# Four 512-token norms worked in two token halves of 256, with the matmuls on either side of them

## The chip, the cores and the metric

The kernel runs on one core of one Trainium2 chip. Inside the core several engines work side by side, each through its own queue of instructions: PE (TensorE: matmuls, with its weight loads shown apart as PEld), DVE (VectorE), ACT (ScalarE), POOL (GpSimd) and SP (SyncE, which issues transfers). They hold each other up only through semaphores. The metric is the time of one execution on the device in microseconds (us); lower is better. The time before is the median of three executions. The profile is of one further execution and has its own, slightly different time.

## The reference

Two blocks run one after the other. The change lies in the second, a trunk of two layers over 256 latent tokens and 256 context tokens, 512 columns in all:

```python
def half_ffn(x, m, name):
    sh, sc, g = m
    h = modulate(rms_norm_2(x, prm[name + "_norm"]), sh, sc)     # h * (1 + sc) + sh
    return x + 0.5 * g * swiglu(h, prm[name + "_w_in"], prm[name + "_w_out"])

def trunk_layer(xl, xc, ...):
    xl = half_ffn(xl, mod_l[0:3], "ffn1");  xc = half_ffn(xc, mod_c[0:3], "ffn1")
    hl = modulate(rms_norm_2(xl, prm["mix_norm"]), mod_l[3], mod_l[4])     # hc the same way
    ol, oc = mixer(hl, hc, ...)                                  # projections, attention, w_out
    xl = xl + mod_l[5] * ol
    xl = half_ffn(xl, mod_l[6:9], "ffn2")                        # xc the same way in layer 0
```

A norm needs the sum of squares of a token's 1024 features before any feature of that token can be scaled. Shift and scale differ between the latent and the context tokens.

## The kernel before

Activations are kept as eight tiles of 128 features by 512 tokens, `x[:, k, :]`. A product is made in three passes over rounded operands: high by high, low by high, high by low. So each weight piece of 128 by 128 costs three matmuls for each of its contraction steps, and both a weight piece and an input tile have to be split first: ACT rounds (`w_hi`, `h_hi`), then DVE takes the difference (`w_lo`, `h_lo`). Weights pass through a ring of four pieces; a piece may be rounded when the piece four places earlier has been multiplied. Accumulators are eight PSUM banks, used in turn.

An FFN works in two halves of its hidden width. Each half first multiplies 22 input pieces (8 contraction steps each) and then 8 output tiles o0 to o7 (11 steps each, three matmuls of 512 columns per step: L1233 to L1235). DVE adds each finished output tile to x (L2368), in two operations of 256 columns. After the last output tile comes the next stage, through a norm:

- ACT squares each x tile (L1581, the last tile in two halves at L1576). PE adds the squares up over features with a column of ones, in small matmuls (`norm_sums`, L991): tiles 0 to 2 after o5, tiles 3 and 4 after o6, the rest after o7. The two accumulators of these sums lie in the banks of o0 and o1.
- For each token half, ACT takes the root (L1589), DVE the reciprocal (L2049), and PE spreads the result over the 128 partitions (`spread_half`, L809, from `rs`).
- DVE multiplies x by it (L2125, halves apart). ACT writes the rounded modulated tile (`h_hi`, L1670) and the unrounded one (L1676), two operations of 256 columns each and one wait for both. DVE subtracts (`h_lo`, L2149).
- PE multiplies the first four weight pieces of the next stage tile by tile as these arrive, 8 steps, three matmuls of 512 columns each, 96 in all: `first_pieces` (L1260, L1261, L1265) where an FFN follows, `first_features` (L875, L876, L878) where a mixer's projections follow. Tiles 0 and 1 come first for all pieces; at the end each piece takes its last steps alone, so piece 0 closes 18 matmuls before the end.
- The weights of pieces 2 and 3 are rounded by ACT in the middle of the modulation (`ahead(2)`, `ahead(3)`; L1742, in the mixers L1648) and split by DVE (L2341, L2183). Piece 4 takes piece 0's place in the ring. In an FFN, ACT's queue has ahead of it a load of an activation table and the SiLU of piece 0's result (L1754); in a mixer, two copies out of PSUM (L1896) and two squares.

Four norms of 512 tokens stand between tiles in this way, in this order of time: "b2.0.nm" (FFN 1 of layer 0, then the mixer), "b2.0.n2" (the mixer's output projection, with 8 steps per tile, then FFN 2), "b2.1.n1" (FFN 2 of layer 0, then FFN 1 of layer 1) and "b2.1.nm" (FFN 1 of layer 1, then its mixer). They are called norms 1 to 4 here. All queues are written out by hand; no scheduler orders them.

Of the kernel before, what the change touches and what calls it, by code (L numbers as in the profile page):

```python
# [196 lines left out]
def columns(items):  # L197
# [26 lines left out]
    "attended", "combined", "copied", "exponentiated", "piece_multiplied", "gated",  # L224
# [91 lines left out]
def program(nc, book, weights, d_const, d_late, d_param, d_cond, d_x, d_ctx, d_bias, d_out):  # L316
# [13 lines left out]
    with ExitStack() as ctx:  # L330
# [33 lines left out]
        mscale = sb("mscale", [P, KD, 2])  # L364
        warm = sb("warm", [P, 1])
# [3 lines left out]
        (attended, combined, copied, exponentiated, piece_multiplied, gated,  # L369
# [217 lines left out]
        NORM_N = {nm: SEQ if nm in ("b1.0", "b1.1", "b2.1.n2") else TOK for nm in BEFORE}  # L587

# [193 lines left out]
        def _(pe):  # L782
# [70 lines left out]

            def first_features(names, rhs, N):
# [183 lines left out]
            def norm(nm, summed_before=0):  # L1038
# [6 lines left out]
                for h in range(halves):  # L1045
                    if E.new(f"{nm}.root.{h}"):
                        pe.wait_ge(*E.at(f"{nm}.root.{h}"))
                    spread_half(f"{nm}.rs.{h}", banks[h], rs, h, SEQ // GROUPS * h)

# [169 lines left out]
            def ffn(nm, nn, N, then=None):  # L1219
# [48 lines left out]

                x_hi, x_lo = [h_hi[:, k, 0:N] for k in range(KD)], [h_lo[:, k, 0:N] for k in range(KD)]
                u_hi, u_lo = [hidden_hi[:, k, 0:N] for k in range(KH)], [hidden_lo[:, k, 0:N] for k in range(KH)]  # L1270
                for half in range(2):
                    tile = tile_number(nm, half)
                    if half == 0:
                        first_pieces()
# [15 lines left out]
                    for o in range(KD):  # L1290
# [6 lines left out]
                        ready = [3 * (tile + k + 1) for k in range(KH)] if o == 0 else None  # L1297
                        piece(half, 2 * KH + o, u_hi, u_lo, ready)
                        if half and then and o in (5, 6):
                            if o == 5:  # L1300
                                state["bank"] = piece_number(nm, 1, 2 * KH) % BANKS
                                for i in range(2):
                                    occupant[(state["bank"] + i) % BANKS] = f"{nm}_o1.{i}"
                            norm_sums(then, range(3) if o == 5 else range(3, 5))
                for o in range(2 * bool(then), KD):
                    q = piece_number(nm, 1, 2 * KH + o)
                    occupant[q % BANKS] = f"{nm}_o1.{o}"
# [125 lines left out]
            norm("b2.0.nm", 5)  # L1433
            rhs = normed("b2.0.nm", TOK)
            state["rotating"] = 7
            for j in range(7):
# [9 lines left out]
                if j == 0:  # L1446
                    first_features([f"b2.0.in.{i}" for i in range(4)], rhs, TOK)
# [44 lines left out]
            for j in range(4):  # L1492
# [3 lines left out]
                if j == 2:  # L1496
                    norm_sums("b2.0.n2", range(4))
            norm("b2.0.n2", 4)
            ffn("b2.0.ffn2", "b2.0.n2", TOK, "b2.1.n1")
            norm("b2.1.n1", 5)  # L1500
# [1372 lines left out]
```

## Time and profile before

| quantity | value |
| --- | --- |
| median of three executions | 2490.09 us (2485.32 to 2491.04) |
| profiled execution, its own time | 2493.8 us |
| span of the profiled execution, first to last instruction | 2492.0 us |
| PE busy | 2417.2 us, 97% of the span |
| DVE busy | 1668.9 us, 67% |
| ACT busy | 993.5 us, 40% |
| DMA | 358.71 MB, mean 144 GB/s |
| mean granted clock of TensorE | 0.979 of full speed |

The profiled execution is 3.7 us above the median, and 1.8 us of it lie outside the span. PE's busy time counts a matmul that runs at a lower granted clock, and one that is stretched by its neighbours, as busy; the share by itself doesn't tell how fast PE works.

### The profile page before, as it was taken

How to read it: one execution, taken by the hardware profiler on the slowest of the kernel's cores; microseconds unless marked ns; L12 is line 12 of the kernel's file. 1: busy time of each engine (PE TensorE's matmuls, PEld its weight loads, DVE VectorE, ACT ScalarE, POOL GpSimd, SP SyncE). 2: the span in 40 equal slices, each digit the busy share in tenths (PEclk: the TensorE clock that was granted, in tenths of full speed). 3: DMA queues.
4: the chain of work that ended last, by engine and by line, in shares of the span. 5: the costliest groups of instructions: out<-in, count | busy, mean ns of one | idle time of the engine just before them, and what ended most of it. 6: DMA issues, size and time to landing. Idle time of an engine off the chain costs nothing.

```text
span 2492.0 us, 38157 instructions
## 1 busy us (share of the span) xinstructions
PE 2417.2 (97%) x15684; PEld 2068.4 (83%) x15684; DVE 1668.9 (67%) x2598; ACT 993.5 (40%) x1493; POOL 50.6 (2%) x72
## 2 busy tenths in 40 slices
PE   8999999999999999999999999999999999998999
PEld 7989899998988888876457888887888887967999
DVE  5589875789868688644864866854856853465654
ACT  5347545366562222252464321225221224455432
POOL 0000000000000000000030000000000000020000
PEclk9999999999999999999989999999999999999999
DMA  7644345544435355413102434432434531502553
GB/s 262 206 168 138 122 148 193 195 173 139 156 109 209 122 201 193 153 68 108 68 1 102 172 135 176 186 126 102 186 131 181 191 115 63 165 18 102 178 188 109
DMA packets 66717, 358.71 MB, mean 144 GB/s; under 512 B 15472, under 2 KB 20720, under 8 KB 30192
## 3 DMA queue, kind: packets, MB, share of 16 engines
q1 hardware_dynamic: 66544, 356.27, 40.0%
q8 instruction: 124, 2.03, 0.3%
q14 instruction: 49, 0.40, 0.0%
HBM read 351.82 MB, written 1.05 MB: 142 GB/s over the span
## 4 chain that ended last, share of the span: by engine, by line
PE 89%; DVE 5%; ACT 3%; issue 1%; POOL 1%; SPq 0%; DMA 0%; DVEq 0%; ACTq 0%; POOLq 0%
PE psum L1233 16%; PE psum L1235 16%; PE psum L1234 16%; PE psum L809 7%; PE psum L846 7%; PE psum L848 7%; PE psum L847 6%; DVE slab L2331 2%; PE psum L924 1%; PE psum L930 1%; PE psum L925 1%; PE psum L1156 1%; PE psum L955 1%; PE psum L957 1%; PE psum L956 1%
## 5 line engine op out<-in xcount | busy, mean ns | idle before, releaser
L1742 ACT ACTIVATE w_hi<-wring 128x1024 fp32r<-128x1024 f32 (+1 forms) x240 | 273.4, 1144 | 531.1 <-PE psum L1235 423.0
L1233 PE MATMUL psum<-h_hi,w_hi 128*128 128x512 f32 (+1 forms) x1280 | 464.4, 363 | 0.7 <-DVE w_lo L2341 0.7
L1234 PE MATMUL psum<-h_lo,w_hi 128*128 128x512 f32 (+1 forms) x1280 | 464.0, 363 | 0.0
L1235 PE MATMUL psum<-h_hi,w_lo 128*128 128x512 f32 (+1 forms) x1280 | 464.0, 363 | 0.0
L2341 DVE TENSOR_TENSOR w_lo<-wring,w_hi 128x1024 fp32r<-128x1024 f32 (+1 forms) x240 | 318.4, 1329 | 151.3 <-ACT w_hi L1742 150.9
L2210 DVE CUSTOM_DVE_ANT_0 products<-wring,cond,prm 128x1024 bf16<-128x1024 f32 x288 | 369.5, 1283 | 7.8 <-DMA wring<-in_w_mod 0.6
L846 PE MATMUL psum<-h_hi,w_hi 128*128 128x256 f32 (+1 forms) x1176 | 355.1, 302 | 10.8 <-issue 8.7
L848 PE MATMUL psum<-h_hi,ring_lo 128*128 128x256 f32 (+1 forms) x1176 | 350.2, 298 | 0.0
L847 PE MATMUL psum<-h_lo,w_hi 128*128 128x256 f32 (+1 forms) x1176 | 349.5, 297 | 0.0
L2183 DVE TENSOR_TENSOR ring_lo<-wring,w_hi 128x1024 fp32r<-128x1024 f32 x208 | 247.2, 1223 | 138.7 <-ACT w_hi L1648 136.5
L1233 PEld LDWEIGHTS psum<-h_hi,w_hi 128*128 128x128 f32 x1280 | 241.6, 189 | 39.1 <-DVE w_lo L2341 1.9
L1234 PEld LDWEIGHTS psum<-h_lo,w_hi 128*128 128x128 f32 x1280 | 241.6, 189 | 37.4
L1235 PEld LDWEIGHTS psum<-h_hi,w_lo 128*128 128x128 f32 x1280 | 241.6, 189 | 37.4
L1233 PE MATMUL psum<-hidden_hi,w_hi 128*128 128x512 f32 (+1 forms) x704 | 255.9, 364 | 0.0
L1234 PE MATMUL psum<-hidden_lo,w_hi 128*128 128x512 f32 (+1 forms) x704 | 255.3, 363 | 0.0
L1235 PE MATMUL psum<-hidden_hi,w_lo 128*128 128x512 f32 (+1 forms) x704 | 255.2, 363 | 0.0
L1648 ACT ACTIVATE w_hi<-wring 128x1024 fp32r<-128x1024 f32 x208 | 211.1, 1053 | 108.7 <-PE psum L848 35.7
L846 PEld LDWEIGHTS psum<-h_hi,w_hi 128*128 128x128 f32 x1176 | 223.4, 190 | 30.1 <-issue 22.6
L847 PEld LDWEIGHTS psum<-h_lo,w_hi 128*128 128x128 f32 x1176 | 224.9, 191 | 6.2
L848 PEld LDWEIGHTS psum<-h_hi,ring_lo 128*128 128x128 f32 x1176 | 224.2, 191 | 6.8
L1754 ACT ACTIVATE squares<-psum 128x512 f32<-128x512 f32 (+1 forms) x88 | 47.9, 544 | 289.9 <-PE psum L1235 289.9
L1233 PEld LDWEIGHTS psum<-hidden_hi,w_hi 128*128 128x128 f32 x704 | 132.9, 189 | 21.0
(211 smaller groups left out, 3525.3 us busy)
## 6 DMA issues: line engine op xcount, KB each, us to landing
wring<-in_w_b_ffn_in SPq DMA_DIRECT2D x80, 1024.0 KB, 6.9
wring<-in_w_mod SPq DMA_DIRECT2D x72, 1024.0 KB, 4.9
wring<-in_w_b_ffn_out SPq DMA_DIRECT2D x64, 704.0 KB, 4.1
wring<-in_w_b_merge SPq DMA_DIRECT2D x24, 1024.0 KB, 4.8
wring<-in_w_b_out SPq DMA_DIRECT2D x16, 1024.0 KB, 4.8
wring<-in_w_b_in SPq DMA_DIRECT2D x16, 1024.0 KB, 5.2
wring<-in_w_b_q SPq DMA_DIRECT2D x12, 1024.0 KB, 6.3
wring<-in_w_b_k SPq DMA_DIRECT2D x12, 1024.0 KB, 5.0
```

The costliest lines, as they stand in the source:

```text
L809: return nc.tensor.matmul(out, lhsT, rhs, start=(k == 0), stop=(k == n - 1))
L846: nc.tensor.matmul(out, mixer_hi(q)[:, k, :], r_hi, start=(k == 0), stop=False)
L847: nc.tensor.matmul(out, mixer_hi(q)[:, k, :], r_lo, start=False, stop=False)
L848: mm = nc.tensor.matmul(out, lo[:, k, P * t:P * t + P], r_hi, start=False, stop=(k == len(rhs) - 1))
L1233: nc.tensor.matmul(acc, wh[:, k, :], rhs_hi[k], start=(k == 0), stop=False)
L1234: nc.tensor.matmul(acc, wh[:, k, :], rhs_lo[k], start=False, stop=False)
L1235: return nc.tensor.matmul(acc, wl[:, k, :], rhs_hi[k], start=False, stop=(k == n - 1))
L1648: A(mixer_hi(q), slot_of(c).rearrange("p (k n) -> p k n", n=256)[:, :, P * i:P * i + P], ACT.Copy).then_inc(weights_rounded, 1)
L1742: A(part_piece(w_hi, q, i), raw_piece(c, i), ACT.Copy).then_inc(weights_rounded, 1)
L2183: V.tensor_tensor(mixer_lo(c)[:, :, P * i:P * i + P], raw, mixer_hi(q).bitcast(F32), ALU.subtract).then_inc(weights_split, 1)
L2210: V.tensor_tensor_reduce(out=products[:, :], in0=slot_of(c)[:, D * t:D * t + D], in1=cond[:, g, :], scale=1.0, scalar=R(f"b2.{l}.mod_b", 2 ...
L2341: V.tensor_tensor(part_piece(w_lo, q, i), raw_piece(c, i), part_piece(w_hi, q, i).bitcast(F32), ALU.subtract).then_inc(weights_split, 1)
```

## The change

The last two output tiles ahead of each of the four norms, the norm, and the first four pieces behind it are worked in two halves of 256 tokens. For each of the norms:

- `last_halves` multiplies o6 and o7 for the first token half, then both for the second, with matmuls of 256 columns (L1130 to L1132). The accumulators hold a half of both tiles each, instead of one tile.
- The sums of squares of tiles 0 to 2 still follow o5, but their accumulators now take the banks of o4 and o5. Tiles 3 to 5 follow the first half of o6. `late_sums` (tiles 6 and 7 of one half) and `spread_root` for the first token half are put into the second half's matmuls, after 12 and 27 of them (24 in norm 2).
- `first_halves` multiplies the first four pieces for the first token half (L1164, L1165, L1167): pieces 0 to 2 step by step, then piece 3 alone. Into it go `late_sums` for the second half after step 2, and `spread_root` for it after step 4. Then follows the second token half in the old order of steps.
- ACT and DVE have `halved_norm` in place of `norm` and `modulate`, and `norm` and `scaled`. Each operation covers one half, with a wait of its own. ACT's squares and root of the second half stand among its operations of the first.
- A separate tile `mgate` keeps the gate factors, which shared `mscale` before.

PE has 630 matmuls more than before: 162 for each of norms 1, 3 and 4, 144 for norm 2.

```diff
+        def halved_base(nm):
+            if nm == "b2.0.n2":
+                return piece_number("b2.0.ffn2", 0) % BANKS
+            return piece_number(HALVED[nm], 1, 2 * KH) % BANKS
+        def halved_banks(nm):
+            free = [(halved_base(nm) + i) % BANKS for i in range(KD - 2)]
...
+            return free[0:PARTS], free[PARTS:]
...
+            def early_sums(nm, some):
+                if some[0] == 0:
+                    state["sum"] = [take(f"{nm}.sum.{h}", fixed=halved_banks(nm)[1][h]) for h in range(2)]
...
+            def last_halves(nm, pieces, accs):
+                for h in range(2):
+                    for p, (w_h, w_l, r_hi, r_lo, close) in enumerate(pieces):
+                        n = len(r_hi)
+                        out = accs[h][:, half_of(p)]
+                        for k in range(n):
+                            nc.tensor.matmul(out, w_h[k], r_hi[k][:, half_of(h)], start=(k == 0), stop=False)
+                            nc.tensor.matmul(out, w_h[k], r_lo[k][:, half_of(h)], start=False, stop=False)
+                            mm = nc.tensor.matmul(out, w_l[k], r_hi[k][:, half_of(h)], start=False, stop=(k == n - 1))
...
+                            if (h, p, k) == (0, 0, n - 1):
+                                early_sums(nm, range(3, KD - 2))
+                            if (h, p, k) == (1, 0, 3):
+                                late_sums(nm, 0)
+                            if (h, p, k) == (1, 0, min(8, n - 1)):
+                                spread_root(nm, 0)
+            def first_halves(nm, lands, weights_of, acc_of, close):
+                first = []
+                for k in range(KD + 1):
+                    first += [(k, i, 0) for i in range(PARTS - 1) if k < KD] + [(k - 1, i, 1) for i in range(PARTS - 1) if k]
+                first += [(k, PARTS - 1, part) for k in range(KD) for part in range(2)]
+                for h, order in enumerate((first, first_passes(TOK))):
...
+                        if (h, k, i, part) == (0, 2, PARTS - 2, 1):
+                            late_sums(nm, 1)
+                        if (h, k, i, part) == (0, 4, PARTS - 2, 1):
+                            spread_root(nm, 1)
...
-                        if half and then and o in (5, 6):
-                            if o == 5:
-                                state["bank"] = piece_number(nm, 1, 2 * KH) % BANKS
...
-                            norm_sums(then, range(3) if o == 5 else range(3, 5))
+                        if half and then and o == 5:
+                            early_sums(then, range(3))
...
+                    last_halves(then, last, [psum[:, piece_number(nm, 1, 2 * KH + o) % BANKS, :] for o in (KD - 2, KD - 1)])
...
+            def halved_norm(nm, l, which, ahead):
...
+                for k in range(KD):
+                    high_and_plain(k, 0)
+                    if k == 1:
+                        ahead(2)
+                    if k == 4:
+                        square(KD - 2, 1)
+                        square(KD - 1, 1)
+                        ahead(3)
+                    if k == 5:
+                        root_half(1)
+                for k in range(KD):
+                    high_and_plain(k, 1)
```

The first place at which rows are shown is PE's queue after output tile o5, ahead of norm 3; L991 and L1030 are the sums of squares, and a name in brackets is a semaphore that the row waits for. Before:

```order
L1235 MATMUL psum<-hidden_hi,w_lo 128x512
L991 MATMUL psum<-squares,cst 32x64 [waits rooted,ffn_added]
L991 MATMUL psum<-squares,cst 32x64 x7
L991 MATMUL psum<-squares,cst 32x64 [waits rooted]
L1233 MATMUL psum<-hidden_hi,w_hi 128x512 [waits weights_split,gated]
L1234 MATMUL psum<-hidden_lo,w_hi 128x512
```

After:

```order
L1360 MATMUL psum<-hidden_hi,w_lo 128x512
L1030 MATMUL psum<-squares,cst 32x64 [waits rooted,ffn_added]
L1030 MATMUL psum<-squares,cst 32x64 x7
L1030 MATMUL psum<-squares,cst 32x64 [waits rooted]
L1130 MATMUL psum<-hidden_hi,w_hi 128x256 [waits hidden_written,weights_split,gated]
L1131 MATMUL psum<-hidden_lo,w_hi 128x256
```

The place of the sums is the same; the `ffn_added` that the first waits for is that of the bank's last tile, o1 before and o5 after, and o6 follows with half the columns.

The second place is PE's queue from the end of o7 to the first weight pieces behind norm 3; L809 is the spreading of the root. Before:

```order
L991 MATMUL psum<-squares,cst 32x64 [waits rooted]
L991 MATMUL psum<-squares,cst 32x64 x3
L809 MATMUL psum<-rs,cst 128x64 [waits ffn_added,normed]
L809 MATMUL psum<-rs,cst 128x64 x3
L809 MATMUL psum<-rs,cst 128x64 [waits ffn_added,normed]
L809 MATMUL psum<-rs,cst 128x64 x3
L1260 MATMUL psum<-h_hi,w_hi 128x512 [waits shifted,weights_split,rooted]
L1261 MATMUL psum<-h_hi,w_lo 128x512
```

After, the same end, and further on the spreading of the second half:

```order
L1131 MATMUL psum<-hidden_lo,w_hi 128x256
L1132 MATMUL psum<-hidden_hi,w_lo 128x256
L1164 MATMUL psum<-h_hi,w_hi 128x256 [waits shifted,weights_split]
L1165 MATMUL psum<-h_hi,w_lo 128x256
L1164 MATMUL psum<-h_hi,w_hi 128x256 [waits weights_split]
```

```order
L1167 MATMUL psum<-h_lo,w_hi 128x256 [waits normed]
L1167 MATMUL psum<-h_lo,w_hi 128x256 x2
L825 MATMUL psum<-rs,cst 128x64 [waits normed,ffn_added]
L825 MATMUL psum<-rs,cst 128x64 x3
L1164 MATMUL psum<-h_hi,w_hi 128x256 [waits shifted]
```

Nothing stands between o7 and the first pieces any more, and a wait for the second half's root stands inside the first pieces.

The third place is ACT's queue in the same norm; L1742 and L1957 round a weight piece, L1670 and L1787 write `h_hi`, L1676 and L1790 the unrounded tile, L1773 squares a half tile and L1779 takes the root of a half. Before:

```order
L1676 ACTIVATE squares<-squares,mods,mscale 128x256
L1742 ACTIVATE w_hi<-wring 128x1024 [waits piece_multiplied,weights_landed2,shifted]
L1670 ACTIVATE h_hi<-squares,mods,mscale 128x256 [waits normed]
L1670 ACTIVATE h_hi<-squares,mods,mscale 128x256
L1676 ACTIVATE squares<-squares,mods,mscale 128x256 [waits shifted]
```

After:

```order
L1773 ACTIVATE squares<-x 128x256 [waits ffn_added,shifted]
L1773 ACTIVATE squares<-x 128x256 [waits ffn_added,rooted]
L1957 ACTIVATE w_hi<-wring 128x1024 [waits piece_multiplied,weights_landed2,rooted]
L1787 ACTIVATE h_hi<-squares,mods,mscale 128x256 [waits normed]
L1790 ACTIVATE squares<-squares,mods,mscale 128x256 [waits shifted]
L1779 ACTIVATE rs<-psum,cst 128x64 [waits summed,shifted]
L1787 ACTIVATE h_hi<-squares,mods,mscale 128x256 [waits normed,rooted]
```

The root of the second half stands behind the first half's tiles 0 to 5, two squares and the rounding of piece 3, and each half operation waits for the one before it.

## Rows read from the trace of the kernel before

**Rows 1.** The page: PE's busy line, and shares of the chain that ended last
```profile
PE 2417.2 (97%) x15684; PEld 2068.4 (83%) x15684; DVE 1668.9 (67%) x2598; ACT 993.5 (40%) x1493; POOL 50.6 (2%) x72
PE 89%; DVE 5%; ACT 3%; issue 1%; POOL 1%; SPq 0%; DMA 0%; DVEq 0%; ACTq 0%; POOLq 0%
```

**Rows 2.** Windows: per norm, o5's end to first pieces, first pieces; busy (x) per engine, PEclk, DMA
```profile
1058.57:1081.65 23.08, 20.45 (x213) 16.15 (x211) 8.12 (x16) 5.51 (x11) 0.15 (x2) 1.00 0.24 92
1081.65:1106.46 24.81, 24.41 (x96) 18.89 (x96) 15.36 (x29) 21.06 (x36) 0.00 (x0) 0.93 0.06 18
1332.91:1351.57 18.66, 16.26 (x194) 12.79 (x193) 8.12 (x16) 5.50 (x11) 0.00 (x0) 1.00 0.42 154
1351.57:1376.25 24.68, 24.05 (x96) 18.91 (x96) 14.04 (x26) 21.53 (x36) 0.00 (x0) 0.93 0.16 55
1698.49:1721.61 23.12, 20.50 (x213) 16.14 (x211) 8.12 (x16) 5.51 (x11) 0.00 (x0) 0.97 0.14 47
1721.61:1746.39 24.78, 24.57 (x97) 19.72 (x97) 14.05 (x26) 21.55 (x36) 0.00 (x0) 0.89 0.13 43
2068.61:2093.57 24.96, 22.09 (x213) 17.73 (x211) 8.12 (x16) 5.51 (x11) 0.00 (x0) 0.90 0.00 1
2093.57:2118.58 25.01, 25.01 (x97) 19.71 (x97) 12.88 (x25) 21.07 (x36) 0.00 (x0) 0.89 0.07 19
```

**Rows 3.** Timeline, norm 3, PE: o7's last matmul to the first piece; start, duration, engine
```profile
1715.33 0.39 PE L1235 MATMUL psum<-hidden_hi,w_lo 128*128 128x512 f32 x1
...
1718.32 2.05 PE L809 MATMUL psum<-rs,cst 128*128 128x64 f32 x16 [0.68 <-DVE rs L2049]
1721.61 0.77 PE L1260 MATMUL psum<-h_hi,w_hi 128*128 128x512 f32 x1 [1.24 <-ACT h_hi L1670]
```

**Rows 4.** Timeline, PE: matmuls of 512 columns (o5, norm 3), and of 256 (a later FFN)
```profile
1689.65 0.39 PE L1235 MATMUL psum<-hidden_hi,w_lo 128*128 128x512 f32 x1
...
1698.49 0.39 PE L1235 MATMUL psum<-hidden_hi,w_lo 128*128 128x512 f32 x1
...
2399.74 0.28 PE L1234 MATMUL psum<-h_lo,w_hi 128*128 128x256 f32 x1
...
2402.98 0.28 PE L1234 MATMUL psum<-h_lo,w_hi 128*128 128x256 f32 x1
```

**Rows 5.** Timeline, norm 1: o5's last matmul, the sums behind it, o5's addition
```profile
1058.57 0.39 PE L1235 MATMUL psum<-hidden_hi,w_lo 128*128 128x512 f32 x1
...
1058.89 0.88 PE L991 MATMUL psum<-squares,cst 128*32 128x64 f32 x48
1059.00 1.00 DVE L2368 SCALAR_TENSOR_TENSOR x<-psum,mscale,x 128x256 f32<-128x256 f32 x2 [0.87 <-PE psum L1235]
```

**Rows 6.** Groups by line, 1690 to 1750 us: ACT's and DVE's half operations; busy, mean ns | idle
```profile
L1670 ACT ACTIVATE h_hi<-squares,mods,mscale 128x256 fp32r<-128x256 f32 x16 | 8.8, 594 | 3.0 <-DVE squares L2125 2.7
...
L1576 ACT ACTIVATE squares<-x 128x256 f32<-128x256 f32 x2 | 0.8, 416 | 7.2 <-PE psum L991 7.1
...
L2049 DVE RECIPROCAL rs<-rs 128x64 f32<-128x64 f32 x2 | 1.0, 524 | 0.7 <-ACT rs L1589 0.7
```

**Rows 7.** Timeline, norm 3: piece 0's last matmul to piece 4's first
```profile
1741.71 0.39 PE L1265 MATMUL psum<-h_lo,w_hi 128*128 128x512 f32 x1
...
1742.16 1.28 ACT L1754 ACT_TABLE_LOAD   x1 [2.26 <-issue]
...
1743.95 2.00 ACT L1742 ACTIVATE w_hi<-wring 128x1024 fp32r<-128x1024 f32 x2
...
1745.11 1.23 DVE L2341 TENSOR_TENSOR w_lo<-wring,w_hi 128x1024 fp32r<-128x1024 f32 x1 [4.40 <-ACT w_hi L1742]
...
1746.39 0.50 PE L1233 MATMUL psum<-h_hi,w_hi 128*128 128x512 f32 x1 [0.21 <-DVE w_lo L2341]
```

**Rows 8.** Timeline, norm 1, PE: piece 0's last matmul, the mixer's next tile's first
```profile
1101.94 0.40 PE L878 MATMUL psum<-h_lo,w_hi 128*128 128x512 f32 x1
...
1107.72 0.47 PE L846 MATMUL psum<-h_hi,w_hi 128*128 128x512 f32 x1 [0.61 <-DVE ring_lo L2183]
```

More of the change, by code:

```diff
@@ new lines, in late_sums, with spread_root @@
+            def late_sums(nm, h):
+                for k in (KD - 2, KD - 1):
+                    if E.new(f"{nm}.sq{k}.{h}"):
+                        pe.wait_ge(*E.at(f"{nm}.sq{k}.{h}"))
+                    mm = half_sums(state["sum"][h], k, h)
+                mm.then_inc(summed, 1)
+                E.step(summed, f"{nm}.c{KD - 1}.{h}")
+            def spread_root(nm, h):
+                per = SEQ // GROUPS
+                acc = take(f"{nm}.rs.{h}", fixed=(halved_base(nm) + KD - 2) % BANKS if h else halved_banks(nm)[1][0])
+                if E.new(f"{nm}.root.{h}"):
+                    pe.wait_ge(*E.at(f"{nm}.root.{h}"))
+                for j in range(GROUPS):
+                    row = C("ident")[:, GW * j:GW * j + 1].broadcast_to([P, P])
+                    mm = product(acc[:, SEQ * h + per * j:SEQ * h + per * j + per], row, rs[:, per * h:per * h + per], 0, 1)
+                mm.then_inc(summed, 1)
+                E.step(summed, f"{nm}.rs.{h}")
@@ L1272, in ffn @@
                     tile = tile_number(nm, half)
-                    if half == 0:
+                    if half == 0 and nn in HALVED:
+                        first_pieces_halved()
+                    elif half == 0:
                         first_pieces()
@@ L1491, in _ @@
             state["rotating"] = BANKS
-            for j in range(4):
+            state["bank"] = halved_base("b2.0.n2")
+            for j in range(3):
                 c, w = next_chunk()
@@ L2343, in split_weights, with ffn @@
                 E.step(weights_split, f"w{c}" if i >= 2 * KH or i % 2 else None)
-            def ffn(nm, l, N, which, ahead=None):
+            def ffn(nm, l, N, which, then=None, ahead=None):
                 def hidden(half, i):
@@ L2396, in ffn, with add_part @@
                         modulations(steps[PIECES * half + i])
-                for o in range(KD - LAG, KD):
-                    if ahead and o >= KD - 2:
-                        ahead(o - KD + 2)
-                    add(1, o)
+                if then is None:
+                    for o in range(KD - LAG, KD):
+                        add(1, o)
+                    return
+                add(1, KD - LAG)
+                for i in range(2):
+                    ahead(i)
+                def add_part(o, g):
+                    q, p = piece_number(nm, 1, 2 * KH + KD - 1), o - KD + 2
+                    if g:
+                        dve.wait_ge(piece_multiplied, q + 1)
+                    elif E.new(f"{then[0]}.half"):
+                        dve.wait_ge(*E.at(f"{then[0]}.half"))
+                    xv = x[:, o, half_of(g)]
+                    V.scalar_tensor_tensor(out=xv, in0=psum[:, (q - 1 + g) % BANKS, half_of(p)], scalar=mgate[:, o, g:g + 1],
+                                           in1=xv, op0=ALU.mult, op1=ALU.add).then_inc(ffn_added, 1)
+                    dve.wait_ge(ffn_added, E.step(ffn_added, f"{nm}_out.x{o}.{g}"))
+                    if p:
+                        E.name_last(f"{nm}_o1.{KD - 2 + g}'")
+                    if g:
+                        E.name_last(f"{nm}_out.x{o}")
+                halved_norm(*then, ahead, add_part)
             def invert(nm):
@@ L2645, in _, with add_mixer @@
             attention("b2.0.att")
-            def add_mixer(nm, l, groups, per, ahead=None):
+            def add_mixer(nm, l, groups, per, then=None, ahead=None):
                 if E.new(f"mod{l}.47"):
                     dve.wait_ge(*E.at(f"mod{l}.47"))
-                for i in range(KD):
-                    if ahead and i >= KD - 2:
-                        ahead(i - KD + 2)
+                for i in range(KD - 2 if then else KD):
                     if i and per == 1 and i <= 4:
```

252 lines of the change are left out of this document (215 added, 37 removed).

## Prediction

> **What bounds the kernel now.** I read the page's busy shares first, then the chain that ended last, then the places that the change touches: a table of windows for the four norms, the timelines of PE, ACT and DVE in norms 1 and 3, and the groups by line there. PE is busy for 97% of the span and carries 89% of the chain, DVE and ACT together 8% [rows 1]. So a norm costs what PE loses in it. The windows give that loss by stage [rows 2]. Stage 1 runs from o5's last matmul to the first matmul of the first four pieces: 23.08, 18.66, 23.12 and 24.96 us for norms 1 to 4. Stage 2 is the first four pieces: 24.81, 24.68, 24.78 and 25.01 us. For stage 1 the reader should see that PE stands nearly still at its end: from o7's last matmul to the first piece are 6.28 us in norm 3 (1715.33 to 1721.61), filled with small sums, the spreading of 2.05 us, and waits of 0.68 us for the reciprocal and 1.24 us for ACT's first tile [rows 3]. For stage 2, the 96 matmuls at the pitch of 0.2267 us (39 of them from 1689.65 to 1698.49 [rows 4]) would need 21.8 us, and 3 us more are used; PE's granted clock is 0.89 to 0.93 there, so part of these matmuls runs at the lower of its two levels, 1.2 GHz. Stage 2 has nearly one length in all four norms although the clock differs: ACT is busy for 21.1 to 21.6 of its 25 us [rows 2]. The pace of ACT and DVE sets it, not PE alone.
>
> **Price of the halves on PE.** At 256 columns the pitch is 0.120 us (27 matmuls from 2399.74 to 2402.98 [rows 4]), so a pair costs 0.240 us where one matmul cost 0.2267: 13.3 ns for each of 630 pairs, 8.4 us in all if nothing else moved. It is contained in the sums below.
>
> The Trainium skill, "TensorE: Matmul & The Clock Gate", section "Back-to-back issue gap", gives the gap of an isolated matmul at the full clock as the columns over 2.4 GHz and 2.5 ns more; by that a pair would cost only 2.5 ns more than one, an estimate of 1.6 us for 630. The rows say 13.3 ns for this kernel's stream, and the sum goes by the rows; with the page's figure it would end 6.8 us lower.
>
> **Stage 1 after, norm 3, counted from o5's last matmul.**
> 1. The sums of tiles 0 to 2 now use the banks of o4 and o5 and wait for DVE's addition of o5. It ends 1.43 us after o5's last matmul starts (1058.57 to 1060.00 [rows 5]); with 0.12 us to start, 1.55 us, where they began after 0.32. All of o6 is queued behind this wait on PE.
> 2. 48 sums at 0.88 us [rows 5], 1.0 with the change of form: 2.55.
> 3. 132 matmuls of o6 and o7 by 0.120: 15.84. The second 48 sums inside them: 1.0.
> 4. Late sums of the first half: 0.5. They wait for two additions (0.5 each) and a square of 0.42 [rows 5, 6], which 12 matmuls just cover. Spreading of one half: half of 2.05 [rows 3], 1.1 with the start; the 15 matmuls ahead of it (1.8 us) cover root and reciprocal. The five changes of form: 0.3.
>
> The sum is 21.3 us. No wait is left at its end: ACT's first tile is ready at 17.3, by step 4. So norms 1 and 3 gain 1.8 us, and norm 4 gains 3.7, since its stage 1 was 1.84 us longer at a granted clock of 0.90 [rows 2]. Norm 2 has 96 matmuls there, 11.5 us: 17.0 against 18.66, a gain of 1.7.
>
> **Stage 2 after, norm 3.**
> 1. 192 matmuls by 0.120: 23.04.
> 2. Late sums of the second half: 0.6, and 0.35 of waiting for their squares, which stand in ACT's queue behind tiles 0 to 4 of the first half.
> 3. Spreading of the second half: 1.1, and a wait. PE reaches it 51 matmuls after the start of the stage, at 21.3 + 6.1 + 1.0 = 28.4. ACT begins the first half's tiles at 17.3 and has ahead of the second root eleven operations of 0.594 us [rows 6] with 0.04 between (7.0), two weight roundings of 1.0 [rows 7] and two squares of 0.42 [rows 6]: 10 us, and about 1 more of waiting for DVE, which works tile by tile with it. The root is then at 28.3; with the reciprocal of 0.52 [rows 6] and the steps between, PE has it at 29.4 to 29.7. Wait: 1.0. PE's remaining matmuls of the first half are queued behind it, and with them every later step of the norm.
> 4. Piece 4. It takes piece 0's ring slot. From piece 0's last matmul follow ACT's table load, SiLU and rounding, and DVE's split, to PE at 1746.39: 4.68 us after 1741.71 [rows 7]. The 18 matmuls behind piece 0 covered 4.08 of it at 0.2267; at 0.120 they cover 2.16. With the next slot and the earlier end of a shorter matmul (0.28 for 0.39 [rows 4]) 2.3 us of waiting are left, where 0.37 were.
>
> The sum is 28.4 against 24.78: 3.6 more. In norms 1 and 4 a mixer follows, and its next tile began 5.78 us after piece 0's last matmul (1101.94 to 1107.72 [rows 8]); 18 matmuls now cover 2.2, so it begins 3.5 us after the last, where it began 1.58 after. Their stage 2 up to that tile is 22.9 + 0.95 + 2.1 + 3.5 = 29.5, against 24.81 + 1.26 = 26.1 and, with the same 1.26, 26.3: 3.4 and 3.2 more. Norm 2 has a wait of its own: piece 2 is needed at the start now, since pieces 0 to 2 go step by step. Its weights are rounded behind the first half's first two tiles, and I add up 9.4 us from the end of o7's first half to the split's end: two additions (1.0), square, root, reciprocal and spreading (2.8 with sums and starts), the product with the root (0.5), three tile operations (1.9), rounding and split (2.3) and the hand-overs. PE is there after 48 matmuls, sums and spreading: 7.9. That is 1.5 us, and 0.3 more at the second root. In the other norms 66 matmuls lie there, and PE comes at 10.1. Norm 2's stage 2 is 30.2: 5.5 more.
>
> **Sum.** Norm 1: +3.4 − 1.8 = +1.6. Norm 2: +5.5 − 1.7 = +3.8. Norm 3: +3.6 − 1.8 = +1.8. Norm 4: +3.2 − 3.7 = −0.5. Together +6.7.
>
> Then the clock. Before, an idle PE at the end of stage 1 was followed by stage 2 at 0.89 to 0.93 [rows 2], and ACT's pace hid that. After, 2.3 to 3.5 us of idle PE end stage 2, ahead of full-width matmuls that nothing else holds back. No row of before shows such a wait there. The bounds are 0 and the 1.84 us that norm 4's stage 1 paid over norm 3's [rows 2]; the two stage 1 differ in nothing else. Before, a wait of this length did lower the clock in each norm, but a stream that is full on both sides is different; I take half, 0.9 for each of four norms: +3.7. The sum is +10.4: 2504.2 for the profiled execution of 2493.8. That execution is 3.7 above the median, and the change is carried over as a difference: 2490.1 + 10.4 = 2500.5.
>
> Edits at no cost: `mgate` is one small operation of DVE in another place; the loads of weights start within a few us of before, and DMA is busy for at most 0.42 of these windows [rows 2]. If a transfer were late after all, it would add to the piece waits.
>
> **Rivals.**
> - A: the new waits leave the clock alone. For it: stage 1 of norm 1 kept 1.00 through its small waits [rows 2]. Against it: the lower clock behind every stage 1. +6.7: 2496.8.
> - C: the clock falls at all four new waits, and in stage 2 at the second root too. For it: stage 2's clock was below 0.94 in all norms [rows 2]. +14.1 without the second and up to +21 with it: 2504 to 2511.
> - D, on the other side: the halves overlap as meant. ACT and DVE are early enough that the second root, the late squares and the next weights are there when PE comes. Stage 2 then takes 23.04 + 0.6 + 1.1 + 0.2 = 24.9, as before, and stage 1's gains remain, 9.0 in all: 2481.4. It decides where the four second stages together add less than 9.0 us, 2.25 per norm. For it: stage 1's gain is sure where the waits of 0.68 and 1.24 go [rows 3]. Against it: the table load, rounding and split behind piece 0 are serial and their length does not depend on the halves [rows 7], while their cover shrinks by 1.92. The Trainium skill, "Perfetto Trace Analysis", section "Optimizing Scalar/DVE Operations", states D's rule: where these engines are not saturated but cause bubbles on others, smaller instructions can bring the end forward; here ACT is close to full in stage 2.
> - That the change doesn't do what it says: PE's rows in its order show the halves and their sums where they are described, so it has no chance of its own.
>
> **How the numbers follow.** The forecast, 2498 to 2503.5, has 0.42; A, 2489 to 2498, 0.30; C 0.20; D 0.08. A measurement of this kernel tells 0.3% from no change, 7.5 us: bounds 2482.6 and 2497.6. Faster is D but for its upper end: 0.07. Within 0.3% are that end and A but for its own: 0.32. Slower are the rest of A, the forecast and C: 0.61. The range leaves out D and the top of C: 2488 to 2509.
>
> **What would show it.** The profile after should have the sums behind o5 starting 1.5 us after its last matmul instead of 0.3; stage 1 of 21.3 (norm 2: 17.0) with no wait at its end; a wait of about 1 us for the reciprocal inside stage 2; a wait of 2.3 us for a split piece ahead of the next full-width tile (3.5 from the last matmul in the mixers), with matmuls behind it at either clock; and norm 2 as the costliest. I am wrong if stage 2 stays at 25 us, or if the waits at its end pull the clock down for longer than one stage.

## The result and the profile after

The changed kernel takes 2495.92 us, the median of 16 runs, against 2489.03 for the kernel before in 16 runs on the same chips: a ratio of 1.0033, with a 95% interval of 1.0025 to 1.0041. It is slower by 6.9 us by the medians, and by 8.2 by the ratio. Its profiled execution took 2497.71 us, with a span of 2495.9.

The page of the profile after, PE's busy line and the chain that ended last, which answer to [rows 1]:

```profile
PE 2415.9 (97%) x16314; PEld 2094.5 (84%) x16314; DVE 1675.1 (67%) x2630; ACT 1003.4 (40%) x1497; POOL 50.4 (2%) x72
PE 88%; DVE 6%; ACT 3%; issue 1%; POOL 1%; SPq 0%; DMA 0%; DVEq 0%; ACTq 0%; POOLq 0%
```

PE has 630 matmuls more and is busy for 1.3 us less; the share says nothing about the loss. The windows of the changed kernel do, as [rows 2] did: per norm, from o5's last matmul to the first piece, and from there to the first matmul of the next full-width tile, with the length, the busy time of PE, its weight loads, DVE, ACT and POOL (instructions in brackets), then the granted clock, and last the DMA share and GB/s:

```profile
1053.69:1074.59 20.90, 19.74 (x255) 18.69 (x254) 7.84 (x14) 7.34 (x12) 0.00 (x0) 1.00 0.26 102
1074.59:1104.14 29.55, 25.84 (x235) 24.36 (x233) 18.34 (x40) 22.30 (x37) 0.15 (x2) 1.00 0.12 41
1331.58:1348.15 16.57, 15.33 (x218) 14.26 (x217) 6.86 (x13) 5.54 (x10) 0.00 (x0) 1.00 0.19 65
1348.15:1378.68 30.53, 25.65 (x219) 24.41 (x217) 16.74 (x36) 23.34 (x38) 0.00 (x0) 1.00 0.28 104
1700.95:1721.92 20.97, 19.75 (x255) 18.69 (x253) 7.83 (x14) 7.34 (x12) 0.00 (x0) 1.00 0.15 52
1721.92:1750.63 28.71, 25.39 (x218) 24.35 (x216) 15.78 (x36) 21.56 (x36) 0.00 (x0) 1.00 0.11 37
2072.90:2093.83 20.93, 19.75 (x254) 18.66 (x253) 7.84 (x14) 7.33 (x12) 0.00 (x0) 1.00 0.00 1
2093.83:2123.38 29.55, 25.86 (x234) 24.37 (x233) 15.86 (x36) 22.31 (x37) 0.00 (x0) 1.00 0.13 42
```

Stage 1 is shorter by 2.2, 2.1, 2.2 and 4.0 us than in [rows 2]. Stage 2, up to the same point before (26.07, 24.68, 24.78 and 26.26 us), is longer by 3.5, 5.9, 3.9 and 3.3. Per norm the change is +1.3, +3.8, +1.8 and −0.7 us, together +6.1. The clock is 1.00 in all eight windows, where stage 2 had 0.89 to 0.93 before.

PE's waits in norm 3, and ahead of it the last matmul and the wait at the end of norm 1, and norm 2's own (timeline of PE; in brackets the idle time just before and what ended it):

```profile
1100.64 0.28 PE L1167 MATMUL psum<-h_lo,w_hi 128*128 128x256 f32 x1
...
1104.14 0.76 PE L862 MATMUL psum<-h_hi,w_hi 128*128 128x512 f32 x1 [2.08 <-DVE ring_lo L2462]
...
1350.28 0.39 PE L1164 MATMUL psum<-h_hi,w_hi 128*128 128x256 f32 x1 [1.48 <-DVE w_lo L2620]
...
1702.55 0.88 PE L1030 MATMUL psum<-squares,cst 128*32 128x64 f32 x48 [1.21 <-DVE x L2647]
...
1730.46 1.08 PE L825 MATMUL psum<-rs,cst 128*128 128x64 f32 x8 [0.85 <-DVE rs L2390]
...
1750.63 0.50 PE L1358 MATMUL psum<-h_hi,w_hi 128*128 128x512 f32 x1 [2.13 <-DVE w_lo L2620]
```

In norm 1, as in norm 4, a wait of 2.08 us for split weights ends the norm. In norm 2 it is a wait of 1.48 for piece 2's weights that the others don't have. The last three stand where the waits of [rows 3] are gone: behind o5 for DVE's addition, inside the first pieces for the second root, and behind them for piece 4's weights.

### The profile page after: what moved, and what is told of

The parts are those of the page before. It is cut to its first block, busy times and chain, and to the rows that moved or that the text cites. A ratio compares the mean times of both kernels' runs of the same rounds, so it can differ in the third digit from the quotient of the medians.

```text
span 2495.9 us, 39502 instructions
## 1 busy us (share of the span) xinstructions
PE 2415.9 (97%) x16314; PEld 2094.5 (84%) x16314; DVE 1675.1 (67%) x2630; ACT 1003.4 (40%) x1497; POOL 50.4 (2%) x72
## 4 chain that ended last, share of the span: by engine, by line
PE 88%; DVE 6%; ACT 3%; issue 1%; POOL 1%; SPq 0%; DMA 0%; DVEq 0%; ACTq 0%; POOLq 0%
PE psum L1358 15%; PE psum L1360 15%; PE psum L1359 15%; PE psum L825 7%; PE psum L862 7%; PE psum L864 6%; PE psum L863 6%; DVE slab L2610 2%; PE psum L963 1%; PE psum L969 1%; PE psum L964 1%; PE psum L1281 1%; PE psum L994 1%; PE psum L996 1%; DVE ring_lo L2462 1%
## 5 line engine op out<-in xcount | busy, mean ns | idle before, releaser
L1957 ACT ACTIVATE w_hi<-wring 128x1024 fp32r<-128x1024 f32 (+1 forms) x240 | 274.0, 1145 | 530.8 <-PE psum L1360 419.7
L1358 PE MATMUL psum<-hidden_hi,w_hi 128*128 128x512 f32 (+1 forms) x638 | 229.5, 360 | 0.0
L1359 PE MATMUL psum<-hidden_lo,w_hi 128*128 128x512 f32 (+1 forms) x638 | 229.5, 360 | 0.0
L1360 PE MATMUL psum<-hidden_hi,w_lo 128*128 128x512 f32 (+1 forms) x638 | 229.5, 360 | 0.0
L1358 PEld LDWEIGHTS psum<-hidden_hi,w_hi 128*128 128x128 f32 x638 | 120.5, 189 | 18.1
```

Of the source, the lines that this page charges most:

```text
L1358: nc.tensor.matmul(acc, wh[:, k, :], rhs_hi[k], start=(k == 0), stop=False)
L1359: nc.tensor.matmul(acc, wh[:, k, :], rhs_lo[k], start=False, stop=False)
L1360: return nc.tensor.matmul(acc, wl[:, k, :], rhs_hi[k], start=False, stop=(k == n - 1))
L1957: A(part_piece(w_hi, q, i), raw_piece(c, i), ACT.Copy).then_inc(weights_rounded, 1)
```

## Experiments

Two theories were set against each other. **W**: each of these waits is a loss by itself, and comes back when what causes it is taken away. **P**: the pace of ACT and DVE sets the norm, so a wait that is taken away returns at the next place. A third came up on the way, the **clock theory**: the granted clock behind a wait costs something of its own. Table early and stagger were run once each, and only their traces are read; the other kernels were timed several times beside the kernel before. Norm lengths below run from o5's last matmul to the next full-width tile; their sum over the four norms is 191.6 us before and 197.7 after.

**Early banks.** The accumulators of the sums lie in banks whose last tiles were added long before.

```diff
-                    state["sum"] = [take(f"{nm}.sum.{h}", fixed=halved_banks(nm)[1][h]) for h in range(2)]
+                    state["sum"] = [take(f"{nm}.sum.{h}", fixed=halved_banks(nm)[0][3 * h]) for h in range(2)]
```

> The changed kernel with one edit: the two accumulators of the sums of squares lie in the banks that pieces 0 and 3 will use (o0 and o3, added long before) instead of those of o4 and o5. Theory W (each of PE's named waits is lost time by itself): the wait of 1.14 to 1.21 us behind o5 goes in all four norms and nothing takes its place, 4.7 us less than the changed kernel, ratio to the kernel before 1.0014. Theory P (ACT's and DVE's pace sets the norm, as it did in stage 2 before): PE comes earlier to waits that grow by as much, 0 to 1 us less, ratio 1.003.

The wait is gone in all four norms, and no other grew: 192.6 us, 5.1 less. In the timeline of PE in norm 3, in a second profile of this kernel, the sums now start 0.32 us after o5's last matmul:

```profile
1701.58 0.39 PE L1360 MATMUL psum<-hidden_hi,w_lo 128*128 128x512 f32 x1
1701.90 0.88 PE L1030 MATMUL psum<-squares,cst 128*32 128x64 f32 x48
```

But the ratio was 1.0029 (1.002 to 1.0039), hardly better than the changed kernel's 1.0033. So W holds for the wait, and not for the time; the ratio is near P's 1.003, but P's way to it, waits that grow by as much, did not come. Both kernels were therefore run side by side once more.

> The changed kernel itself once more, on the same chip as the next run. Its four norms take 197.7 us again. Clock theory: where PE's granted clock falls outside the norms differs from one profile to the next, so the span differs by some us with the same norms; the ratio to the kernel before is 1.0033 again (1.002 to 1.0045).

> The early banks alone once more, beside the changed kernel. Theory W: 5.1 us less than the changed kernel beside it (its norms are shorter by that), a ratio lower by 0.0021. Clock theory: its waits of 2.1 us at the end of the pieces are followed by stretches at 1.2 GHz in norms 2 and 3, as in its first trace and unlike the changed kernel, and the ratio is lower by only 0.0004 to 0.001.

The ratios were 1.0028 (1.0017 to 1.0038) for the changed kernel and 1.0026 (1.0015 to 1.0038) for the early banks, with the same norms again (197.6 and 192.6 us). The windows of the 6 us behind the end of each norm show where it went. The changed kernel, first profile (norms 1 to 4; the number before the last two is the granted clock), and behind it norms 2 and 3 of its second profile:

```profile
1104.14:1110.14 6.00, 6.00 (x19) 4.83 (x20) 3.35 (x3) 3.87 (x5) 0.00 (x0) 0.72 0.38 157
1378.68:1384.68 6.00, 6.00 (x26) 4.96 (x27) 5.86 (x9) 2.13 (x4) 0.00 (x0) 1.00 0.34 105
1750.63:1756.63 6.00, 6.00 (x26) 4.96 (x27) 5.86 (x9) 2.13 (x4) 0.00 (x0) 1.00 0.38 112
2123.38:2129.38 6.00, 6.00 (x19) 4.82 (x20) 3.36 (x3) 3.87 (x5) 0.00 (x0) 0.72 1.11 243
...
1378.51:1384.51 6.00, 6.00 (x26) 4.98 (x27) 5.86 (x9) 2.15 (x4) 0.00 (x0) 1.00 0.38 109
1750.41:1756.41 6.00, 6.00 (x26) 4.99 (x27) 5.86 (x9) 2.18 (x4) 0.00 (x0) 1.00 0.37 105
```

And the early banks, second profile, and behind it norms 2 and 3 of the first:

```profile
1103.92:1109.92 6.00, 6.00 (x19) 4.77 (x20) 3.35 (x3) 3.86 (x5) 0.00 (x0) 0.72 0.35 147
1377.78:1383.78 6.00, 6.00 (x19) 4.84 (x20) 5.86 (x9) 1.94 (x3) 0.00 (x0) 0.72 0.33 102
1749.97:1755.97 6.00, 6.00 (x19) 4.79 (x20) 5.86 (x9) 1.94 (x3) 0.00 (x0) 0.72 0.33 111
2123.02:2129.02 6.00, 6.00 (x20) 4.81 (x21) 3.35 (x3) 3.87 (x5) 0.00 (x0) 0.76 1.11 239
...
1379.36:1385.36 6.00, 6.00 (x19) 4.81 (x20) 5.86 (x9) 1.95 (x3) 0.00 (x0) 0.72 0.35 108
1751.59:1757.59 6.00, 6.00 (x19) 4.81 (x20) 5.86 (x9) 1.95 (x3) 0.00 (x0) 0.72 0.33 106
```

PE makes 26 matmuls in 6 us at 2.4 GHz and 19 where part of them runs at 1.2 GHz: seven fewer, 1.6 us at the pitch of 0.2267. In the changed kernel norms 2 and 3 end with the same wait of 2.13 us and no fall of the clock, in both of its profiles; with the early banks the clock falls behind them, in both of its profiles. That is 3.2 us of the 5.1. The rest of the two profiled spans, outside the norms, where the instructions are the same, is longer by more than that: 2305.8 and 2304.0 us with the early banks, 2298.2 and 2295.3 in the changed kernel. But these two executions of the early banks are among their slowest, 2500.26 us where the median of ten is 2494.59 and 2498.40 where the median of twelve is 2492.97. By the medians of the side-by-side run, less the 1.8 us outside the span and the norms, the rest is 2298.6 against 2295.3 us, and 3.3 us is about what the two falls cost. Executions of the same mean granted clock do differ as the norms say: at 0.988 the changed kernel's spans there are 2491.1 and 2492.0 us, those of the early banks 2486.5 and 2487.6. So the early banks' gain is real in the norms, and most of it was lost outside them, 3.2 us of it by the two falls.

**Closing early.** In the second token half each piece takes its last four steps alone, so piece 0 closes 36 matmuls before the end instead of 18.

```diff
-                for h, order in enumerate((first, first_passes(TOK))):
+                second = [p for p in first_passes(TOK) if p[0] < KD - 4]
+                second += [(k, i, part) for i in range(PARTS) for k in range(KD - 4, KD) for part in range(2)]
+                for h, order in enumerate((first, second)):
```

> The changed kernel with another order of the second token half of the first four pieces: each piece takes its last four steps alone, so piece 0 closes 36 matmuls (4.3 us) before the end instead of 18 (2.2 us). Theory W: the wait of 2.13 us for piece 4's weights goes in norms 2 and 3, and 2.1 us of the wait ahead of the mixer's next tile in norms 1 and 4: 8.4 us less than the changed kernel; the matmuls at 1.2 GHz behind the mixers' waits (8 each, 1.6 us) should return to 2.4 GHz with it, 3 us more: ratio to the kernel before 0.9987 to 1.000. Theory P: ACT and DVE do not have the last tiles of the second half by then, and a wait inside the half takes its place: under 3 us, ratio above 1.002.

The norms take 189.2 us, 8.5 less, as W said (8.4). In norm 3 no idle time is left ahead of the next tile (timeline of PE):

```profile
1742.40 0.28 PE L1169 MATMUL psum<-h_lo,w_hi 128*128 128x256 f32 x1
1742.66 0.50 PE L1360 MATMUL psum<-h_hi,w_hi 128*128 128x512 f32 x1
```

The ratio was 1.0008 (0.9999 to 1.0017): some 6 us less than the changed kernel by the ratios, against the 8.4 to 11.4 that W gave. ACT and DVE had the last tiles in time, and P falls here; the size fell short of W.

**Closing late**, the opposite: the pieces take the last two steps in turn, and piece 0 closes 9 matmuls before the end.

```diff
+                second = [p for p in first_passes(TOK) if p[0] < KD - 2]
+                second += [(k, i, part) for k in range(KD - 2, KD) for i in range(PARTS) for part in range(2)]
```

> The opposite of the run before: the pieces take the last two steps in turn, so piece 0 closes 9 matmuls (1.1 us) before the end. Theory W: the wait behind the first pieces is a fixed chain less its cover, and grows by 9 times 0.12 in each norm, 4.3 us more than the changed kernel, ratio 1.005; in norms 2 and 3 it shows 3.2 us ahead of the next tile. Theory P: no change within 1 us.

The wait ahead of piece 4 is the predicted 3.2 us (timeline of PE, norm 3):

```profile
1759.98 0.79 PE L1360 MATMUL psum<-h_hi,w_hi 128*128 128x512 f32 x1 [3.21 <-DVE w_lo L2622]
```

The norms take 201.9 us, 4.2 more, as W said. The ratio was 1.0079 (1.0067 to 1.0092), 11 us more than the changed kernel and not 4.3: outside the norms its profile, the slowest of its five executions, took 2307.0 us, the longest of all, at the lowest granted clock of the experiments, 0.981. The clock fell behind all four norms, and in two of them for longer than in the changed kernel (the 6 us behind each):

```profile
1107.98:1113.98 6.00, 6.00 (x15) 4.70 (x16) 3.35 (x3) 3.86 (x5) 0.00 (x0) 0.52 0.28 116
1385.35:1391.35 6.00, 6.00 (x19) 4.76 (x20) 5.86 (x9) 1.95 (x3) 0.00 (x0) 0.72 0.36 108
1759.98:1765.98 6.00, 6.00 (x15) 4.70 (x16) 5.86 (x9) 1.94 (x3) 0.00 (x0) 0.52 0.32 111
2136.41:2142.41 6.00, 6.00 (x19) 4.82 (x20) 3.35 (x3) 3.87 (x5) 0.00 (x0) 0.72 1.04 230
```

Against 26 matmuls at the full clock 36 are missing in the four windows, 8 us, where the changed kernel's first profile lost 3.2. So most of what came on top of the norms lies right behind them.

**Table early.** One small ACT operation of the gate's function behind norms 2 and 3, so that the table load stands where ACT is idle.

```diff
+                if nm in ("b2.0.n2", "b2.1.n1"):
+                    A(warm[:, :], C("eps"), ACT.Silu).then_inc(rooted, 1)
+                    act.wait_ge(rooted, E.step(rooted))
```

> The changed kernel with one small ACT operation behind the norm in norms 2 and 3, of the function that the gate uses, so that the table load of 1.28 us stands where ACT is idle and not behind piece 0. Theory W: the wait for piece 4's weights falls from 2.13 to 0.85 us in these two norms, and stays 2.08 ahead of the mixers. Rival (the wait is for the transfer of the weights or for DVE): it stays 2.13.

The load ends before piece 0 closes, and the wait falls to 0.86 in norm 3, 0.86 in norm 2 (timelines of ACT and PE in norm 3):

```profile
1739.67 1.28 ACT L1811 ACT_TABLE_LOAD   x1
...
1743.53 0.60 ACT L1972 ACTIVATE squares<-psum 128x512 f32<-128x512 f32 x1 [2.36 <-issue]
...
1746.45 0.50 PE L1358 MATMUL psum<-h_hi,w_hi 128*128 128x512 f32 x1 [0.86 <-DVE w_lo L2623]
```

The wait fell by 1.27 us for a load of 1.28, so it isn't the transfer of the weights, as the rival had it. With the two runs before it this shows that the wait is a chain from piece 0's close less the matmuls behind piece 0, with the table load in the chain; that SiLU, rounding and split are its other links is read from the trace and was not varied.

**Later root.** The second half's late sums and its root stand one step later in the first half of the pieces.

```diff
-                        if (h, k, i, part) == (0, 2, PARTS - 2, 1):
+                        if (h, k, i, part) == (0, 3, PARTS - 2, 1):
-                        if (h, k, i, part) == (0, 4, PARTS - 2, 1):
+                        if (h, k, i, part) == (0, 5, PARTS - 2, 1):
```

> The changed kernel with the second half's late sums behind step 3 instead of 2 of the first half of the first pieces, and the spreading of its root behind step 5 instead of 4. Theory W: the waits of 0.20, 0.20 and 0.85 us inside the first pieces go, up to 5 us less than the changed kernel in four norms, ratio 1.0013 to 1.002. Theory P: the second half's tiles come at the same time as before, and the time goes into a wait at the start of the second half: 0 to 1 us, ratio 1.003.

The waits of 0.20 and 0.85 are gone, and two others have come, for ACT's tiles 5 and 6 of the first half, the two that stand behind the squares, the rounding of piece 3 and the root in ACT's queue (timeline of PE, norm 3):

```profile
1722.56 0.39 PE L1164 MATMUL psum<-h_hi,w_hi 128*128 128x256 f32 x1 [0.77 <-ACT h_hi L1787]
...
1724.42 0.39 PE L1164 MATMUL psum<-h_hi,w_hi 128*128 128x256 f32 x1 [0.53 <-ACT h_hi L1787]
```

The norms take 196.4 us, 1.3 less in place of 5. Here P is nearer, though its place was another: inside the first half, and not at the start of the second. The ratio was 1.0028 (1.0017 to 1.0039).

**Stagger.** In norm 2 alone, piece 2 stays two steps behind pieces 0 and 1.

```diff
+                late = 2 if nm == "b2.0.n2" else 0
+                for step in range(KD + 1 + late):
+                    for part in range(2):
+                        for i in range(PARTS - 1):
+                            k = step - part - (late if i == PARTS - 2 else 0)
+                            if 0 <= k < KD:
+                                first.append((k, i, part))
```

> The changed kernel with piece 2 two steps behind pieces 0 and 1 in norm 2 alone. Theory W: the wait of 1.48 us for piece 2's weights goes, norm 2 is 45.6 us from o5 to the next tile instead of 47.1. Theory P (in norm 2 ACT's first half sets the pace anyway): the wait goes, and waits for ACT's tiles or for the second root take 1 us or more of it back.

The wait for the weights is gone, and three waits for ACT's tiles take its place, 3.73 us in all (timeline of PE, norm 2):

```profile
1353.86 0.39 PE L1169 MATMUL psum<-h_hi,w_hi 128*128 128x256 f32 x1 [0.65 <-ACT h_hi L1792]
...
1358.41 0.39 PE L1169 MATMUL psum<-h_hi,w_hi 128*128 128x256 f32 x1 [1.95 <-ACT h_hi L1792]
...
1362.06 0.58 PE L1169 MATMUL psum<-h_hi,w_hi 128*128 128x256 f32 x1 [1.13 <-ACT h_hi L1792]
```

Norm 2 takes 50.9 us, 3.8 more than in the changed kernel. P is right in that waits for ACT's tiles took back all that went. But they don't make the 3.8: all waits of the norm sum to 7.1 us where they were 6.1. The rest came with the clock, which fell inside the norm (the windows of the whole norm, and of the stretch behind the wait of 1.95):

```profile
1333.69:1384.56 50.87, 43.74 (x434) 41.04 (x433) 23.61 (x49) 28.76 (x47) 0.00 (x0) 0.93 0.23 84
1358.80:1365.60 6.80, 5.67 (x40) 5.21 (x40) 2.75 (x7) 2.91 (x6) 0.00 (x0) 0.50 0.44 154
```

Nor is the third wait ACT's pace: the late sums are placed by piece 2's steps, so the edit moved them back with it, and ACT stood idle for 2.07 us ahead of the second root, at 1361.07, for PE's sums.

**Early banks and closing early together**, and then with the later root as well:

> The edits of the early banks and of the early closing together, on the changed kernel. Theory W with the clock (a wait costs its length, and ahead of full-width matmuls it may also be followed by a stretch at 1.2 GHz, whose cost is not the wait's): 5.1 us of the first, which it lost again behind the waits at the end of the pieces when it stood alone, and 8 us of the second now add up, since no wait of 2 us is left: 5 us less than the run with early closing alone, ratio to the kernel before 0.9988 (0.998 to 0.9997). Theory P: ACT's tiles take over, ratio 1.0005 or above.

> The run with both edits and, besides, the later sums and root. Theory W: 1.3 us less than without (what the later root brought in the four norms of its own trace), ratio 0.998. Theory P, inside the first half of the pieces: waits for ACT's tiles 6 and 7 of 0.87 and 0.53 us in each norm as in that trace, and a further wait in the second half for its last tiles, which piece 0 now needs 18 matmuls earlier: 0 to 1 us more than without.

The first took 2479.47 us, a ratio of 0.9967 (0.9955 to 0.998), the second 2477.73, 0.9957 (0.994 to 0.9973). Both beat both kernels. In the second the waits for ACT's tiles (5 and 6 once more) come back as P said, up to 0.87 and 0.53 us, but its further wait in the second half doesn't, and the norms are 1.2 us shorter, as W said; the times of the two are too close to tell apart. Their norms take 184.2 and 183.0 us: 13.5 less than the changed kernel for the two edits together, 5.1 + 8.5 to within 0.2, and 1.2 less again with the later root. The time fell by more, 15 to 16 us by the ratios, from 1.003 to 0.9967, and more than expected: 13.5 us of norms and the 1.6 to 3.2 that the falls behind them cost make 15.1 to 16.7. No wait of 2 us is left in a norm, and the windows of 6 us behind the norms show 1.00 in all four, here in the last kernel:

```profile
1102.15:1108.15 6.00, 6.00 (x26) 4.87 (x27) 3.35 (x3) 4.01 (x6) 0.00 (x0) 1.00 0.49 178
1369.22:1375.22 6.00, 6.00 (x27) 4.95 (x27) 5.86 (x9) 2.13 (x4) 0.00 (x0) 1.00 0.35 106
1737.41:1743.41 6.00, 6.00 (x27) 4.98 (x27) 5.86 (x9) 2.15 (x4) 0.00 (x0) 1.00 0.33 104
2106.53:2112.53 6.00, 6.00 (x28) 4.92 (x29) 3.35 (x3) 4.02 (x6) 0.00 (x0) 1.00 0.88 260
```

One table sums up the profiled executions: the norms by their timelines, and the rest of the span, in which the instructions are the same.

| kernel | span, us | four norms | rest | mean granted clock |
| --- | --- | --- | --- | --- |
| before | 2492.0 | 191.6 | 2300.4 | 0.979 |
| changed | 2495.9 | 197.7 | 2298.2 | 0.985 |
| changed, again | 2492.9 | 197.6 | 2295.3 | 0.987 |
| early banks | 2498.4 | 192.6 | 2305.8 | 0.982 |
| early banks, again | 2496.6 | 192.6 | 2304.0 | 0.983 |
| closing early | 2485.6 | 189.2 | 2296.4 | 0.987 |
| closing late | 2508.9 | 201.9 | 2307.0 | 0.981 |
| later root | 2490.8 | 196.4 | 2294.4 | 0.989 |
| table early | 2491.4 | 195.0 | 2296.4 | 0.986 |
| stagger | 2501.3 | 201.4 | 2299.9 | 0.985 |
| early banks, closing early | 2477.2 | 184.2 | 2293.0 | 0.988 |
| all three | 2476.3 | 183.0 | 2293.3 | 0.989 |

Each row is one execution, and executions of one kernel differ by some 10 us: the 16 of the changed kernel have spans from 2489.8 us at a mean granted clock of 0.989 to 2499.3 at 0.984. Among the kernels with halves the rest follows the clock, from 2293 us at 0.988 and 0.989 to 2307 at 0.981. The kernel before stands apart, with 2300.4 at 0.979, because part of its lower clock lies inside its norms, where ACT's pace hides it [rows 2].

## Why the prediction was right

The direction and the range were right, and the sum of the norms nearly so: 6.7 us predicted, 6.1 measured. The forecast's own narrow interval, 2498 to 2503.5 with a chance of 0.42, was missed: the measured 2495.92 lies in A's.

- **Stage 1.** 21.3 predicted, 20.90 to 20.97 measured; norm 2 17.0 and 16.57. The wait behind o5 is 1.14 to 1.21 us, and o6 queues behind it as described. The 0.3 us for changes of form was not needed. No wait is left at its end. The pitch was as priced: 630 pairs at the 12 ns measured below are 7.6 us, an estimate and more than the norms' whole 6.1, so the time that the halves saved and the new waits nearly cancel.
- **Stage 2.** 28.4 predicted for norm 3, 28.71 measured; norm 2 30.2 and 30.53; norms 1 and 4 29.5 and 29.55. The waits: late sums 0.35 predicted, one or two of 0.20 measured; second root 1.0 and 0.85; piece 4 2.3 and 2.13; piece 2 in norm 2 1.5 and 1.48; the mixer's next tile in norm 1 3.5 after the last matmul, and 3.50 (1100.64 to 1104.14). ACT's chain was priced to the second root's end at 28.3 us; in norm 3 it ended at 28.3, with ACT busy from 1725.70 to it but for gaps of 0.03. That this chain makes the root late fits the later root, which moved the wait to ACT's tiles; that the end is a fixed chain with less cover is shown by the two orders and the table load.
- **The clock** is the mis-sized term. I took 0.9 us behind each of four waits, half of 1.84, 3.7 in all. It came or it did not: in the first profile 1.6 us behind norms 1 and 4 and nothing behind 2 and 3, in the second, by the same windows, a fall behind norm 1 alone. So it was 3.2 and 1.6. As a mean the half was fair: of the 26 waits of 2.08 and 2.13 us at the ends of the norms, in all the profiles but that of closing late, 16 were followed by a fall. The forecast of +10.4 was 3.5 above the measured +6.9 (2.2 above the ratio's 8.2), and its 2500.5 stands 4.6 above the measured median, of which 1.1 is the median of the kernel before, now 2489.03 with more runs.
- **What the sum left out** is the clock in the rest of the span. Between the first two profiles the rest fell by 2.2 us although it holds the two new falls behind the norms. By the medians it is 2295.6 us before and 2296.4 after, an estimate that takes the norms' lengths from the profiles: the falls of 1.6 to 3.2 were in part made up elsewhere. That the total came out close to the norms' own sum is in that part luck. A difference of profiles can't be read as the norms' doing for that reason; the norms' own timelines can.
- **Rivals.** A's 2496.8 lies closest to the measured time, but not by its mechanism: the clock did fall behind two waits. C did not happen in the changed kernel; closing late came to its price, 2506.26 us, and the clock did fall behind all four norms there, but its norms are also 4.2 us longer, so this is no test of the price. The early banks had all four falls too. D, that the halves overlap as meant, needed stage 2 to add less than 2.25 us per norm, and it added 3.3 to 5.9. The combined kernels show that D was two or three edits away: once the sums had free banks and piece 0 closed earlier, the norms were 7.4 and 8.6 us shorter than before, where D had 9.0, and the ratios make them 8.2 and 10.7 us faster. (9.0 off 2490.1 is 2481.1; D's 2481.4 doesn't follow from it.)
- **The rule of the Trainium skill on the gap of matmuls** ("TensorE: Matmul & The Clock Gate", "Back-to-back issue gap") is for an isolated matmul, and the section says that in a stream the weight loads count too; the estimate from it was 2.5 ns more for a pair. The trace disagrees with the estimate: 30 steps of 256 columns took 3.58 us (1056.25 to 1059.83), 0.119 each, 12 ns more per pair than the 0.2267 of [rows 4]. The measurement decides. The other rule of the Trainium skill ("Perfetto Trace Analysis", "Optimizing Scalar/DVE Operations") says that smaller operations can bring the end forward. No run here tests it by itself: ACT's tile operations had 256 columns before too [rows 6], and stage 1, shorter by 2.1 to 4.0 us per norm, changed PE's order as well.

What stays open: why the clock falls behind a wait of 2.13 us with the early banks and not in the changed kernel. The two differ ahead of it only in the wait of 1.2 us behind o5, at the start of the norm. Nor do instructions and waits alone decide it: behind norm 4 the changed kernel shows a clock of 0.72 in one profile and 1.00 in the other. And closing early alone measured some 6 us where its norms and the windows behind them gave 8.5 or more; by the medians its rest was 2298.2 us, where the changed kernel had 2296.4 and 2295.3.

## What to carry to other kernels

Working a stage in halves shortens what the engine stood still for, and shortens by as much what covered the fixed chains beside it: count, for each chain that doesn't shrink (a table load, a rounding, a split), how many matmuls still lie over it, and put the operation that starts it earlier. A buffer that is chosen because it is free last brings a wait of its own. A wait on a busy PE should be priced with and without a lower clock behind it. In these profiles, over the 6 us behind a norm, a fall followed none of 14 with 0.86 us of waiting or less ahead of the next tile, 16 of 26 with 2.08 or 2.13, and 4 of 4 in closing late, which waited longest.

## What the runs showed of the hardware

The same wait of 2.13 us ahead of the same instructions was followed by a granted clock of 1.00 in one kernel and 0.72 in another over the next 6 us, each in two profiles of two. And the rest of this kernel, the same instructions outside the norms, took 2293 to 2307 us in the kernels with halves, longer where the mean granted clock was lower (0.989 to 0.981): more than the whole change moved.
